# Final norm and the first projections behind an MLP, made by halves of the positions, the second half first

## The chip, the cores and the metric

The kernel runs on one core of one Trainium2 chip. The metric is the device time of one execution in microseconds; smaller is better. The kernel before took 2222.27 us in the median of 3 runs (2221.69 to 2226.16).

## The reference, cut to what matters

Two blocks run one after the other on 1024 positions of 1024 channels in float32. The first ends with a squared-ReLU MLP, its residual, and a norm; the second begins with a norm, a modulation and a wide input projection. Between the two stands the part that the change touches:

```python
h = h + squared_relu_mlp(rms_norm(h, mlp_norm[i]), mlp_w_up[i], mlp_w_down[i])
return rms_norm(h, final_norm)                       # end of the first block
...
h = _modulate(_rms(x, norm1_g[l]), sh1, sc1)         # h * (1 + scale) + shift
p = h @ w_in[l]                                      # 512 of its columns feed _fourier
...
y = jnp.fft.fft2(fg, axes=(1, 3), norm="ortho").real # positions x 128 channels, 4 groups
```

## The kernel before, in words

**Data.** Activations lie transposed: channels on the 128 partitions in 8 blocks, positions along the free dimension. `X` is the residual, 8 blocks of 1024 positions; "half 0" is positions 0 to 511 and "half 1" 512 to 1023, which is also what one PSUM bank of 512 float32 holds. Every large matmul is written as three (lines 99 to 101), on operands that are split into a `hi` part (made by ScalarE, "ACT") and a `lo` part (made by VectorE, "DVE"). `U` is the normed and modulated input of the projections, as such a pair.

**The end of the MLP.** The down projection runs as 7 passes of 8 steps, s = 0 to 55. A step is 4 blocks d of 6 matmuls, 24 in all. The four blocks of a pass accumulate in banks 0 to 3 or in banks 4 to 7, in turn: the sixth pass (s = 40 to 47) in 0 to 3, the last one (s = 48 to 55) in 4 to 7. Steps 54 and 55 are interleaved, block by block, so that block d of the last pass is done after 12 matmuls each. DVE makes the lo parts of the weights three steps ahead of TensorE (`make_lo`), and in its own step s = 48 + d adds block d of the sixth pass to `X` from its bank (`evict`, line 1765, two instructions). In the same steps ACT squares finished blocks of `X` (twice, plain and with the gain `GF`), and DVE adds the squares up in `sq` and `sqg` (line 1774). Half 1 of `X` is complete earlier than half 0: its squares belong to steps 41 to 45, those of half 0 to steps 49 to 52 and to the four blocks of the last pass.

**The norm.** `final_pe` sums the squares over channels by matmul (line 1855, 16 short ones a half; one matmul of float32 in the program is two instructions on TensorE), ACT takes roots (line 1873), DVE makes a diagonal matrix of the reciprocals (lines 1914, 1916), and a matmul with ones turns it into a row of 512 factors on all partitions (line 1862). Then for each of the 8 blocks of `X`: `t` on DVE (`X` times scale times row, line 1903), `hi` on ACT (plus shift, line 1868), `lo` on DVE (line 1908). All of that stands behind the last matmul of the MLP. Block 0 is made by halves, blocks 1 to 7 at full width.

**The projections and the Fourier part.** `four_pe` projects four groups g of 128 channels with the weight tiles `T_F[g]`: 48 matmuls for a group, 24 for one half. It makes groups 0 and 1 together, chunk by chunk as `U` comes, then group 2, then `over_channels(0)` and `(1)`, group 3, and from there position and channel transforms in turn. ACT and DVE feed them in fixed orders: ACT copies one bank of a group (`second`, line 1995), DVE folds, ACT and DVE split the result (line 2001), and so on. Behind it the gates' projections begin.

**What sets the order.** Each engine runs its list in program order; a wait on a semaphore stops all that is behind it on that engine. A PSUM bank is taken by `claim(pe, b)`, which waits for the marks that `hand_over(b, ...)` left when the bank was last filled. The queue of SyncE loads weight tiles as their buffers come free, GpSimd's queue stores finished blocks of `X` and loads small tables.

Of the kernel before, what the change touches and what calls it, by code (L numbers as in the profile page):

```python
# [103 lines left out]
def _program(nc, A, out, ctx):  # L104
# [1648 lines left out]
    def down_dve(dve):  # L1753
# [91 lines left out]

    def u_mark(k, i=1):
        return fn.dve("lo", 0, i) if k == 0 else fn.dve("lo", k)

    def final_pe(pe):
        for i in range(2):  # L1850
            claim(pe, fs_b[i])
            for name, s, c, w in (("n3", sq[0], 0, INV_EPS), ("n3g", sqg[0], 1, INV1024)):
                pe.wait_ge(*ml.dve(name, "add", i, 7))
                for tb in range(4):
                    m = pe.e.matmul(psum[:, fs_b[i], 2 * tb + c:2 * tb + 2], s[:, (4 * i + tb) * P:(4 * i + tb + 1) * P],
                                    w, start=(c, tb) == (0, 0), stop=(c, tb) == (1, 3), skip_group_check=True)
            m.then_inc(*fn.pe.one("sums", i))
            hand_over(fs_b[i], 1, fn.act("sd1", i))
        claim(pe, f_rb, 2)
        for i in range(2):  # L1860
            pe.wait_ge(*fn.dve("dg", i))
            pe.e.matmul(bank(f_rb + i), ones[:], dg[:, 4 * i:4 * i + 4, :].rearrange("p a b -> p (a b)"),
                        start=True, stop=True).then_inc(*fn.pe.one("row", i))
        hand_over(f_rb, 2, fn.dve("t", 7))

    def final_act(act):
        def hi(k, x, *step):
            act.e.activation(U[0][:, k, x], tmp[k % 2][:, x], ACT.Identity, bias=SH1[:, k:k + 1]).then_inc(
                *fn.act.one("hi", k, *step))

        for i in range(2):
            act.wait_ge(*fn.pe("sums", i))
            act.e.activation(s2[:, 4 * i:4 * i + 4], psum[:, fs_b[i], 1:8:2], ACT.Sqrt, bias=EPSEPS).then_inc(
                *fn.act.one("sd", i))
        for i in range(2):
            act.wait_ge(*fn.dve("t", 0, i))
            hi(0, half(i), i)
        for i in range(2):
            act.e.activation(s1[:, 4 * i:4 * i + 4], psum[:, fs_b[i], 0:8:2], ACT.Sqrt, bias=EPSV).then_inc(
                *fn.act.one("sd1", i))  # L1880
        for k in range(1, 8):
            act.wait_ge(*fn.dve("t", k))
            hi(k, slice(0, 1024))
# [14 lines left out]

    def final_dve(dve):
        e = dve.e  # L1900

        def t(k, x, *step):
            e.scalar_tensor_tensor(tmp[k % 2][:, x], X[:, k, x], SCF[:, k:k + 1], two(f_rb)[:, x], ALU.mult,
                                   ALU.mult).then_inc(*fn.dve.one("t", k, *step))

        def lo(k, x, *step):
            dve.wait_ge(*fn.act("hi", k, *step))
            e.scalar_tensor_tensor(U[1][:, k, x], tmp[k % 2][:, x], SH1[:, k:k + 1], f(U[0][:, k, x]), ALU.add,
                                   ALU.subtract).then_inc(*fn.dve.one("lo", k, *step))

        for i in range(2):
            c = slice(4 * i, 4 * i + 4)
            dve.wait_ge(*fn.act("sd", i))
            e.reciprocal(r2[:, c], s2[:, c]).then_inc(*fn.dve.one("rs", i))
            dve.wait_ge(*fn.dve("rs", i))
            e.tensor_tensor(dg[:, c, :], ident_rows(4), by_block(r2[:, c], 4), ALU.mult).then_inc(
                *fn.dve.one("dg", i))
        for i in range(2):
            dve.wait_ge(*fn.pe("row", i))
            t(0, half(i), i)  # L1920
        lo(0, half(0), 0)
        for k in range(1, 9):
            if k < 8:
                if k > 1:
                    dve.wait_ge(*u_mark(k - 2))
                t(k, slice(0, 1024))
            if k == 1:
                lo(0, half(1), 1)
                dve.wait_ge(*fn.act("sd1", 1))
                e.reciprocal(r1, s1).then_inc(*fn.dve.one("r1"))  # L1930
            else:
                lo(k - 1, slice(0, 1024))
# [35 lines left out]
    def four_pool(pool):  # L1968
# [180 lines left out]
    def four_pe(pe):  # L2149
# [26 lines left out]
        def project(g):  # L2176
            w = use(pe, T_F[g])
            claim(pe, g_b[g], 2)
            for i in range(2):
                for k in range(8):  # L2180
                    m = mm3(pe.e, bank(g_b[g] + i), cols(w, k, 128), ch(U, k, 512 * i, 512 * i + 512), k == 0, k == 7)
            m.then_inc(*fo.pe.one("f", g))

        ws = [use(pe, T_F[g]) for g in range(2)]
        for g in range(2):
            claim(pe, g_b[g], 2)
        for k in range(8):
# [1872 lines left out]
```

## Time and profile before

| what | value |
|---|---|
| median of 3 runs | 2222.27 us |
| the profiled execution | 2221.08 us |
| its span | 2219.0 us |
| TensorE busy | 2143.2 us, 97% |
| DVE busy | 1634.1 us, 74% |
| ACT busy | 1123.2 us, 51% |

The chain that ended last is TensorE for 82% of the span, DVE for 10% and ACT for 5%. "PEclk" in a view is the granted clock of TensorE as a share of 2.4 GHz: 1.00 is that, 0.50 is 1.2 GHz. In a timeline a matmul of 512 columns shows 0.39 us, but one starts every 0.227 us at the full clock: the starts tell the pace.

### The profile page before, as it was taken

The page shows a single profiled execution, that of the slowest core. Times are in us where ns is not written, and L with a number is a line of the kernel's source. Part 1 is how long each engine was busy: PE and PEld are TensorE (multiplying, and loading weights), DVE is VectorE, ACT ScalarE, POOL GpSimd, SP SyncE. Part 2 cuts the span into 40 slices and gives each one's busy share as a digit, 9 for nine tenths or more (in the row PEclk, how much of TensorE's full clock was granted, in tenths as well). Part 3 has the DMA queues.
Part 4 walks back from the last instruction along what each step waited for, and adds up shares of the span by engine and source line. Part 5 has one row for each costly group of instructions (what it writes and reads, how often), then busy time and mean ns, then how long its engine had stood idle before and what let it go on. Part 6 is the DMA issues. An engine that isn't in the chain of part 4 may idle for free.

```text
span 2219.0 us, 28129 instructions
## 1 busy us (share of the span) xinstructions
PE 2143.2 (97%) x10948; PEld 1789.3 (81%) x10948; DVE 1634.1 (74%) x2537; ACT 1123.2 (51%) x1725; POOL 188.3 (8%) x269
## 2 busy tenths in 40 slices
PE   8999999999999999999999999999998999899997
PEld 6898787788888888878888988788887885688885
DVE  7777457988987987986343263688887746699996
ACT  6777435444443434444322242576766312588874
POOL 0011100000001000000110032000000100111111
PEclk9999999999999999989999999999999999899998
DMA  4122712644469998652343112000001703899996
GB/s 151 48 68 85 258 74 89 216 170 176 179 242 400 384 336 281 221 127 76 124 143 99 38 48 82 10 1 1 1 20 39 280 29 141 345 392 384 378 384 221
DMA packets 114532, 373.99 MB, mean 169 GB/s; under 512 B 13360, under 2 KB 13648, under 8 KB 112736
## 3 DMA queue, kind: packets, MB, share of 16 engines
q1 hardware_dynamic: 86544, 273.00, 33.5%
q0 software_dynamic: 26704, 95.01, 13.1%
q10 hardware_dynamic: 1152, 4.19, 0.5%
q8 instruction: 86, 1.41, 0.3%
q14 instruction: 46, 0.38, 0.1%
HBM read 302.94 MB, written 69.21 MB: 168 GB/s over the span
## 4 chain that ended last, share of the span: by engine, by line
PE 82%; DVE 10%; ACT 5%; issue 1%; DMA 1%; POOLq 0%; SPq 0%; ACTq 0%; DVEq 0%
PE psum L99 24%; PE psum L100 24%; PE psum L101 24%; PE psum L3008 3%; PE psum L3019 2%; DVE w_lo L281 2%; ACT MP_hi L3109 1%; ACT PB L3075 1%; PE psum L1017 1%; DVE MP_lo L3202 1%; PE psum L990 1%; DVE small L3155 1%; PE psum L3848 1%; PE psum L3575 1%; DVE idx L3548 1%
## 5 line engine op out<-in xcount | busy, mean ns | idle before, releaser
L272 ACT ACTIVATE w_hi<-rawe 128x1024 fp32r<-128x1024 f32 x211 | 217.8, 1056 | 152.7 <-PE psum L101 78.7
L99 PE MATMUL psum<-U_hi,w_hi 128*128 128x512 f32 x688 | 271.7, 395 | 12.2 <-DVE w_lo L281 10.5
L281 DVE TENSOR_TENSOR w_lo<-rawe,w_hi 128x1024 fp32r<-128x1024 f32 x211 | 249.5, 1218 | 37.5 <-ACT w_hi L272 37.0
L100 PE MATMUL psum<-U_lo,w_hi 128*128 128x512 f32 x688 | 269.9, 392 | 0.0
L101 PE MATMUL psum<-U_hi,w_lo 128*128 128x512 f32 x688 | 269.3, 391 | 0.0
L281 DVE TENSOR_TENSOR w_lo<-raw,w_hi 128x1024 fp32r<-128x1024 f32 (+2 forms) x175 | 194.5, 1120 | 87.6 <-ACT w_hi L272 87.3
L272 ACT ACTIVATE w_hi<-raw 128x1024 fp32r<-128x1024 f32 (+2 forms) x176 | 169.0, 967 | 92.3 <-PE psum L101 55.5
L99 PE MATMUL psum<-B_hi,w_hi 128*128 128x512 f32 x448 | 176.2, 393 | 6.0 <-ACT cbuf L1433 4.3
L100 PE MATMUL psum<-B_lo,w_hi 128*128 128x512 f32 x448 | 175.3, 391 | 0.0
L101 PE MATMUL psum<-B_hi,w_lo 128*128 128x512 f32 x448 | 175.3, 391 | 0.0
L99 PE MATMUL psum<-w_hi 128*128 128x512 f32 x448 | 174.3, 389 | 0.0
L100 PE MATMUL psum<-w_lo,w_hi 128*128 128x512 f32 x448 | 174.3, 389 | 0.0
L101 PE MATMUL psum<-w_hi,w_lo 128*128 128x512 f32 x448 | 174.3, 389 | 0.0
L99 PEld LDWEIGHTS psum<-U_hi,w_hi 128*128 128x128 f32 x688 | 130.2, 189 | 39.4 <-DVE w_lo L281 10.7
L101 PEld LDWEIGHTS psum<-U_hi,w_lo 128*128 128x128 f32 x688 | 130.2, 189 | 28.0
L100 PEld LDWEIGHTS psum<-U_lo,w_hi 128*128 128x128 f32 x688 | 130.3, 189 | 25.2 <-issue 0.2
L3202 DVE TENSOR_TENSOR MP_lo<-psum,MP_hi 128x512 fp32r<-128x512 f32 x160 | 109.5, 685 | 53.6 <-ACT MP_hi L3109 53.0
L3109 ACT ACTIVATE MP_hi<-psum 128x512 fp32r<-128x512 f32 x160 | 95.6, 597 | 82.7 <-PE psum L3008 82.3
L3008 PE MATMUL psum<-ident,PB 128*128 128x128 f32 x640 | 100.4, 280 | 9.3 <-DVE MP_lo L3202 4.9
L99 PE MATMUL psum<-w_hi,xe_hi 128*128 128x512 f32 x256 | 103.9, 406 | 3.7 <-DVE hv L3803 2.7
L99 PEld LDWEIGHTS psum<-B_hi,w_hi 128*128 128x128 f32 x448 | 84.7, 189 | 24.5 <-issue 5.0
L3008 PEld LDWEIGHTS psum<-ident,PB 128*128 128x128 f32 x640 | 73.8, 141 | 35.1 <-DVE MP_lo L3202 9.4
(490 smaller groups left out, 5135.6 us busy)
## 6 DMA issues: line engine op xcount, KB each, us to landing
rawe<-in_w_e SPq DMA_DIRECT2D x112, 512.0 KB, 17.5
rawe<-in_w_dn SPq DMA_DIRECT2D x70, 512.0 KB, 6.4
rawx<-in_w_e SPq DMA_DIRECT2D x56, 512.0 KB, 18.0
rawe<-ta SPq DMA_DIRECT2D x43, 512.0 KB, 7.3
ta<-cbuf SPq DMA_DIRECT2D x64, 256.0 KB, 2.5
raw<-in_w_dn SPq DMA_DIRECT2D x26, 512.0 KB, 6.5
ta<-rg SPq DMA_DIRECT2D x48, 256.0 KB, 2.0
raw<-in_w_e SPq DMA_DIRECT2D x24, 512.0 KB, 17.6
```

What stands on the lines that cost most here:

```text
L99: e.matmul(o, l[0], r[0], start=first, stop=False, skip_group_check=skip)
L100: e.matmul(o, l[0], r[1], start=False, stop=False, skip_group_check=skip)
L101: return e.matmul(o, l[1], r[0], start=False, stop=last, skip_group_check=skip)
L272: act.e.activation(hi, src, ACT.Copy).then_inc(w_hi, 1)
L281: dve.e.tensor_tensor(lo, src, f(hi), ALU.subtract).then_inc(w_lo, 1)
L990: m = pe.e.transpose(bank(B_T[u % 2], 256 * h + P * i, 256 * h + P * i + P), EX[j % 2][:, s + i, h, P - P * i:2 * P - P * i], ident[:])
L1017: m = pe.e.matmul(psum[:, B_L + h, o + c0:o + 256], qst[(j + 1) % 2][h][:, n * P:n * P + P], kst[h][x][:, k0:n * P + P], start=x == 0, sto ...
L3008: m = pe.e.transpose(bank(t_bank("turn", n), 256 * kb + P * i, 256 * kb + P * i + P), PB[(2 * u + i) % 5][:, (2 * t + kb) * P:(2 * t + kb ...
L3019: m = pe.e.matmul(bank(B_MO, 0, 256), VV[:, 2 * y + kb, v // 4, :], MP[n0 % 4][x][:, 256 * kb:256 * kb + 256], start=(y, kb, x) == (0, 0, ...
L3075: act.e.activation(PB[m % 5][:], s_of(m), ACT.Exp, bias=nmx[:, m % 8:m % 8 + 1], accum_out=msum(c)[:, z:z + 1]).then_inc(*at_s.act.one("ex ...
L3109: act.e.activation(MP[n % 4][0][:], bank(t_bank("turn", n)), ACT.Copy).then_inc(*at_s.act.one("turn", n))
L3202: dve.e.tensor_tensor(lo[:], bank(t_bank("turn", n)), f(hi[:]), ALU.subtract).then_inc(*at_s.dve.one("turn", n))
```

## The change

- **Sums and row of half 1 move into the last pass.** `final_sums(pe, 1)` stands ahead of step 52, `final_row(pe, 1)` ahead of the interleaved steps 54 and 55. ACT's roots follow its squares of step 52, DVE's diagonal its sums of step 52. Both halves' sums now use one bank, 2; the row of half 1 uses bank 0, that of half 0 bank 6.
- **`U` is made by halves**, half 1 first, with buffers `th` of 512 in place of `tmp` of 1024. Four chunks of half 1 are made between the last evictions of the MLP, the other four behind them, then the eight of half 0.
- **The projections are made by halves.** Groups 0 and 1 of half 1 together, with the sums of half 0 behind chunk 3; the row of half 0; groups 2 and 3 of half 1; then half 0 of groups 0, 1, 2, the two channel transforms, and half 0 of group 3.
- **The tiles `T_F[2]` and `T_F[3]`** are split inside the norm, not behind it. The groups' banks change from 4, 6, 2, 0 to 2, 4, 6, 0.
- The table for the root is loaded by ACT in step 51, not ahead of the last squares.

```diff
@@ down_act
+            if s == 51:
+                act.e.activation(vec[:, 122:123], EPSV, ACT.Sqrt)
+            if s == 52:
+                final_root(act, 1)
+        u_hi(act, 0, 1)
+        u_hi(act, 1, 1)
         for d in range(4):
-            if d == 3:
-                act.e.activation(vec[:, 122:123], EPSV, ACT.Sqrt)
             squares(0, 4 + d)
+            if d < 2:
+                u_hi(act, 2 + d, 1)
@@ down_dve
+            if s == 52:
+                final_diag(dve, 1)
+        u_t(dve, 0)
+        u_t(dve, 1)
+        u_lo(dve, 0)
         for d in range(4):
             evict(6, d, 0)
             adds(0, 4 + d)
+            if d < 2:
+                u_t(dve, 2 + d)
+                u_lo(dve, 1 + d)
+            if d == 1:
+                u_lo(dve, 3)
@@ down_pe
         for s in range(N_S - 2):
+            if s == 52:
+                final_sums(pe, 1)
             for d in range(4):
                 m = step(s, d, s % 8)
...
+        final_row(pe, 1)
@@ the norm
-    g_b = [4, 6, 2, 0]
-    f_rb, fs_b = g_b[3], (g_b[2], g_b[2] + 1)
+    g_b = [2, 4, 6, 0]
+    f_rb, fs_b = (6, 0), 2
+    th = [at(f"th{i}", [512], O_V + (44 + 2 * i) * KB) for i in range(2)]
+    U_ORDER = [(k, i) for i in (1, 0) for k in range(8)]
...
+    def final_sums(pe, i):
+        claim(pe, fs_b)
+        for name, s, c, w in (("n3", sq[0], 0, INV_EPS), ("n3g", sqg[0], 1, INV1024)):
+            pe.wait_ge(*ml.dve(name, "add", i, 7))
+            for tb in range(4):
+                m = pe.e.matmul(psum[:, fs_b, 2 * tb + c:2 * tb + 2], s[:, (4 * i + tb) * P:(4 * i + tb + 1) * P],
+                                w, start=(c, tb) == (0, 0), stop=(c, tb) == (1, 3), skip_group_check=True)
+        m.then_inc(*fn.pe.one("sums", i))
+        hand_over(fs_b, 1, fn.act("sd1", i))
+
+    def final_row(pe, i):
+        claim(pe, f_rb[i])
+        pe.wait_ge(*fn.dve("dg", i))
...
+    def project(pe, gs, i, after=None):
+        ws = [use(pe, T_F[g]) for g in gs]
+        for g in gs:
+            claim(pe, g_b[g] + i)
+        for k in range(8):
+            pe.wait_ge(*u_mark(k, i))
+            for g, w in zip(gs, ws):
+                m = mm3(pe.e, bank(g_b[g] + i), cols(w, k, 128), ch(U, k, 512 * i, 512 * i + 512), k == 0, k == 7)
+            if after and k == 3:
+                after(pe, 0)
+        return m
+
     def final_pe(pe):
...
+        project(pe, (0, 1), 1, final_sums)
+        final_row(pe, 0)
+        project(pe, (2,), 1)
+        project(pe, (3,), 1)
...
+    def u_hi(act, k, i):
+        act.wait_ge(*fn.dve("t", k, i))
+        if (k, i) == (0, 1):
+            act.wait_ge(*ml.pe("d", 52))
+        if (k, i) == (4, 1):
+            act.wait_ge(*ml.pe("dn", 6, 3))
+        act.e.activation(U[0][:, k, half(i)], th[k % 2][:], ACT.Identity, bias=SH1[:, k:k + 1]).then_inc(
+            *fn.act.one("hi", k, i))
...
     def final_act(act):
+        u_hi(act, 4, 1)
+        u_hi(act, 5, 1)
+        make_hi(act, T_F[2])
+        u_hi(act, 6, 1)
+        u_hi(act, 7, 1)
+        final_root(act, 0)
+        make_hi(act, T_F[3])
+        for k in range(8):
+            u_hi(act, k, 0)
...
+    def u_t(dve, n):
+        k, i = U_ORDER[n]
+        if k == 0:
+            dve.wait_ge(*fn.pe("row", i))
+        if n > 1:
+            dve.wait_ge(*u_mark(*U_ORDER[n - 2]))
+        dve.e.scalar_tensor_tensor(th[n % 2][:], X[:, k, half(i)], SCF[:, k:k + 1], bank(f_rb[i]), ALU.mult,
+                                   ALU.mult).then_inc(*fn.dve.one("t", k, i))
...
     def final_dve(dve):
+        u_t(dve, 4)
+        for n in range(5, 8):
+            u_t(dve, n)
+            u_lo(dve, n - 1)
+        u_lo(dve, 7)
+        make_lo(dve, T_F[2])
+        final_diag(dve, 0)
+        make_lo(dve, T_F[3])
+        u_t(dve, 8)
+        for n in range(9, 16):
+            u_t(dve, n)
+            u_lo(dve, n - 1)
...
@@ the Fourier part
-        pool.wait_ge(*fn.pe("sums", 1))
+        pool.wait_ge(*fn.pe("sums", 0))
         pool.e.dma_start(cdr[:], A["dft_c"]).then_inc(cd_in.sem, 16)
...
-        project(2)
+        for g in range(3):
+            project(pe, (g,), 0).then_inc(*fo.pe.one("f", g))
         over_channels(0)
         over_channels(1)
-        project(3)
+        project(pe, (3,), 0).then_inc(*fo.pe.one("f", 3))
```

On TensorE, at the border between steps 51 and 52, the kernel before has (`w_hi` and `w_lo` are the split weights and activations; rows with `w_hi` on both sides belong to the MLP, and the second row is the first of step 52):

```order
L101 MATMUL psum<-w_hi,w_lo 128x512
L99 MATMUL psum<-w_hi 128x512 [waits w_lo_made]
L100 MATMUL psum<-w_lo,w_hi 128x512
L101 MATMUL psum<-w_hi,w_lo 128x512
L99 MATMUL psum<-w_hi 128x512
```

and the changed kernel, at the same place:

```order
L101 MATMUL psum<-w_hi,w_lo 128x512
L1879 MATMUL psum<-vec,sq_102 128x2 [waits mlp_dve]
L1879 MATMUL psum<-vec,sq_102 128x2 x3
L1879 MATMUL psum<-vec,sqg_179 128x1 x4
L99 MATMUL psum<-w_hi 128x512 [waits w_lo_made]
```

The sums of half 1 now stand between the two steps, with one wait on a count of DVE's (`mlp_dve`), and every matmul of the MLP behind them is queued behind that wait.

On DVE, from the sums of step 52 (the first two rows) to the second block of the last pass, the kernel before has:

```order
L1774 TENSOR_TENSOR sq_102<-sq_102,sq_103 128x512 [waits mlp_dve,mlp_act]
L1774 TENSOR_TENSOR sqg_179<-sqg_179,sqg_180 128x512 [waits mlp_dve,mlp_act]
L1774 TENSOR_TENSOR sq_102<-sq_102,sq_104 128x512 [waits mlp_dve,mlp_act]
L1774 TENSOR_TENSOR sqg_179<-sqg_179,sqg_180 128x512 [waits mlp_dve,mlp_act]
L281 TENSOR_TENSOR w_lo<-raw_61,w_hi 128x1024 [waits w_hi_made]
L281 TENSOR_TENSOR w_lo<-raw_59,w_hi 128x1024 [waits w_hi_made]
L1765 TENSOR_TENSOR X<-X,psum 128x512 [waits mlp_products]
```

and the changed kernel, from the diagonal that follows the same two rows:

```order
L1953 RECIPROCAL st<-st 128x4 [waits final_norm_act]
L1955 TENSOR_TENSOR dg<-ident,st 128x512 [waits final_norm_dve]
L1780 TENSOR_TENSOR sq_102<-sq_102,sq_104 128x512 [waits mlp_dve,mlp_act]
L1780 TENSOR_TENSOR sqg_179<-sqg_179,sqg_180 128x512 [waits mlp_dve,mlp_act]
L281 TENSOR_TENSOR w_lo<-raw_61,w_hi 128x1024 [waits w_hi_made]
L281 TENSOR_TENSOR w_lo<-raw_59,w_hi 128x1024 [waits w_hi_made]
L1964 SCALAR_TENSOR_TENSOR th_181<-X,modb,psum 128x512 [waits final_norm_products]
L1964 SCALAR_TENSOR_TENSOR th_182<-X,modb,psum 128x512
L1970 SCALAR_TENSOR_TENSOR U_lo<-th_181,mod,U_hi 128x512 [waits final_norm_act]
L1771 TENSOR_TENSOR X<-X,psum 128x512 [waits mlp_products]
```

The diagonal came in ahead of the last sums of a step, and two `t` and a `lo` between the weight tiles and the first eviction of the last pass.

## Rows read from the trace of the kernel before

**Rows 1.** Timeline of TensorE: start us, us, engine line op names [idle <-releaser].

```profile
940.80 0.39 PE L99 MATMUL psum<-w_hi 128*128 128x512 f32 x1
...
962.34 0.39 PE L101 MATMUL psum<-w_hi,w_lo 128*128 128x512 f32 x1
966.65 1.02 PE L1855 MATMUL psum<-vec,sq 128*128 128x2 f32 x8 [3.93 <-DVE sq L1774]
...
972.53 3.76 PE L1862 MATMUL psum<-dg,ones 128*128 128x512 f32 x4
977.89 0.77 PE L99 MATMUL psum<-U_hi,w_hi 128*128 128x512 f32 x1 [1.59 <-DVE U_lo L1908]
```

**Rows 2.** Windows there: length, PE, PEld, DVE, ACT, POOL busy (x), PEclk, DMA, GB/s.

```profile
967.00:968.00 1.00, 1.00 (x10) 1.00 (x10) 0.12 (x1) 0.00 (x0) 0.00 (x0) 0.84 0.75 299
...
981.00:982.00 1.00, 1.00 (x5) 0.84 (x4) 1.00 (x1) 1.00 (x1) 1.00 (x2) 0.83 0.00 0
```

**Rows 3.** Timeline of DVE in the last pass (columns as Rows 1).

```profile
942.62 1.28 DVE L1765 TENSOR_TENSOR X<-X,psum 128x512 f32<-128x512 f32 x2
...
954.32 2.35 DVE L281 TENSOR_TENSOR w_lo<-raw,w_hi 128x1024 fp32r<-128x1024 f32 x2
956.60 0.68 DVE L1765 TENSOR_TENSOR X<-X,psum 128x512 f32<-128x512 f32 x1
957.97 0.69 DVE L1774 TENSOR_TENSOR sq<-sq,sq 128x512 f32<-128x512 f32 x1 [0.70 <-ACT sq L1725]
```

**Rows 4.** Timeline of ACT in the last pass.

```profile
951.94 2.01 ACT L272 ACTIVATE w_hi<-raw 128x1024 fp32r<-128x1024 f32 x2 [1.44 <-PE psum L101]
...
963.77 1.28 ACT L1744 ACT_TABLE_LOAD   x1
965.06 0.20 ACT L1744 ACTIVATE vec<-vec 128x1 f32<-128x1 f32 x1
```

**Rows 5.** Instructions on tile tmp: durations ns min/median/max, starts, forms.

```profile
L1903 DVE SCALAR_TENSOR_TENSOR tmp<-X,modb,psum x9: 747/1280/1281, 974.6 to 992.2; 128x1024 f32<-128x1024 f32 x7, 128x512 f32<-128x512 f32 x2
L1868 ACT ACTIVATE U_hi<-tmp,mod x9: 722/1154/1157, 975.4 to 993.5; 128x1024 fp32r<-128x1024 f32 x7, 128x512 fp32r<-128x512 f32 x2
L1908 DVE SCALAR_TENSOR_TENSOR U_lo<-tmp,mod,U_hi x9: 744/1279/1284, 977.0 to 994.7; 128x1024 fp32r<-128x1024 f32 x7, 128x512 fp32r<-128x512 f32 x2
```

**Rows 6.** Timeline of TensorE, an earlier norm: sums, then two rows.

```profile
345.63 1.95 PE L420 MATMUL psum<-vec,sq 128*128 128x1 f32 x16
...
368.47 1.88 PE L1623 MATMUL psum<-n2dg,ones 128*128 128x512 f32 x4
```

**Rows 7.** Timeline of TensorE, two other gaps.

```profile
351.06 0.76 PE L99 MATMUL psum<-B_hi,w_hi 128*128 128x512 f32 x1 [3.48 <-ACT cbuf L1433]
...
1929.71 0.47 PE L99 MATMUL psum<-w_hi,xe_hi 128*128 128x512 f32 x1 [2.72 <-DVE hv L3803]
```

**Rows 8.** Windows around these two gaps (columns as Rows 2).

```profile
349.00:350.00 1.00, 0.00 (x0) 0.00 (x0) 1.00 (x3) 1.00 (x3) 0.00 (x0) 0.94 0.63 225
...
356.00:357.00 1.00, 1.00 (x5) 0.77 (x4) 1.00 (x3) 0.20 (x1) 0.00 (x0) 0.65 0.00 0
...
1930.00:1931.00 1.00, 1.00 (x4) 0.84 (x3) 0.59 (x1) 0.00 (x0) 0.00 (x0) 0.62 1.02 406
...
1933.00:1934.00 1.00, 1.00 (x5) 0.77 (x4) 0.66 (x1) 0.31 (x1) 0.00 (x0) 0.67 1.01 401
```

**Rows 9.** Timeline of the Fourier part, ACT's rows and the gates' first matmul.

```profile
1001.61 0.60 ACT L1995 ACTIVATE f2nd<-psum 128x512 f32<-128x512 f32 x1 [4.75 <-PE psum L101]
...
1005.14 1.06 ACT L2001 ACTIVATE FF_hi<-ff 128x1024 fp32r<-128x1024 f32 x1 [0.85 <-DVE ff L2085]
...
1007.93 1.06 ACT L2001 ACTIVATE FF_hi<-ff 128x1024 fp32r<-128x1024 f32 x1 [1.12 <-DVE ff L2085]
...
1009.49 1.99 ACT L272 ACTIVATE w_hi<-raw 128x1024 fp32r<-128x1024 f32 x2
1012.49 0.60 ACT L1995 ACTIVATE f2nd<-psum 128x512 f32<-128x512 f32 x1 [1.01 <-PE psum L101]
1012.98 0.17 ACT L2010 ACTIVATE small<-psum 128x3 f32<-128x3 f32 x1
...
1046.34 0.40 PE L99 MATMUL psum<-U_hi,w_hi 128*128 128x512 f32 x1
```

More of the change, by code:

```diff
@@ L1844, in _program @@
-    s1, r1, s2, r2 = (st[:, i, 0:8] for i in range(4))
-    def u_mark(k, i=1):
-        return fn.dve("lo", 0, i) if k == 0 else fn.dve("lo", k)
-    def final_pe(pe):
[L1850 to L1864, printed above, removed]
@@ L1866, in final_act @@
-    def final_act(act):
[L1867 to L1883, printed above, removed]
+    g_b = [2, 4, 6, 0]
@@ new lines, in _program @@
+    f_rb, fs_b = (6, 0), 2
+    th = [at(f"th{i}", [512], O_V + (44 + 2 * i) * KB) for i in range(2)]
+    U_ORDER = [(k, i) for i in (1, 0) for k in range(8)]
+    fn.pe.plan(("sums", 1), ("row", 1), ("sums", 0), ("row", 0))
+    fn.act.plan(("sd", 1), ("sd1", 1), *[("hi", k, 1) for k in range(8)], ("sd", 0), ("sd1", 0),
+                *[("hi", k, 0) for k in range(8)])
+    fn.dve.plan(*[("mod", i) for i in range(6)], ("scf",), ("rs", 1), ("dg", 1))
+    for n, y in enumerate(U_ORDER):
+        if n == 8:
+            fn.dve.plan(("rs", 0), ("dg", 0))
+        fn.dve.plan(("t", *y))
+        if n % 8 and n != 4:
+            fn.dve.plan(("lo", *U_ORDER[n - 1]))
+        if n in (3, 7, 15):
+            fn.dve.plan(("lo", *y))
@@ new lines, in final_row @@
+    def final_row(pe, i):
+        claim(pe, f_rb[i])
+        pe.wait_ge(*fn.dve("dg", i))
+        pe.e.matmul(bank(f_rb[i]), ones[:], dg[:, 4 * i:4 * i + 4, :].rearrange("p a b -> p (a b)"),
+                    start=True, stop=True).then_inc(*fn.pe.one("row", i))
+        hand_over(f_rb[i], 1, fn.dve("t", 7, i))
+    def project(pe, gs, i, after=None):
[9 more added lines that the diff above has]
+        return m
@@ new lines, in final_pe, with final_root @@
+    def final_pe(pe):
+        project(pe, (0, 1), 1, final_sums)
+        final_row(pe, 0)
+        project(pe, (2,), 1)
+        project(pe, (3,), 1)
+    def final_root(act, i):
+        c = slice(4 * i, 4 * i + 4)
+        act.wait_ge(*fn.pe("sums", i))
+        act.e.activation(s2[:, c], psum[:, fs_b, 1:8:2], ACT.Sqrt, bias=EPSEPS).then_inc(*fn.act.one("sd", i))
+        act.e.activation(s1[:, c], psum[:, fs_b, 0:8:2], ACT.Sqrt, bias=EPSV).then_inc(*fn.act.one("sd1", i))
+    def u_hi(act, k, i):
[6 more added lines that the diff above has]
+            *fn.act.one("hi", k, i))
@@ L1897, in modulation @@
         e.tensor_tensor(SCF, SC1, GF, ALU.mult).then_inc(*fn.dve.one("scf"))
-    def final_dve(dve):
[L1900 to L1932, printed above, removed]
@@ new lines, in u_lo @@
+    def u_lo(dve, n):
+        k, i = U_ORDER[n]
+        dve.wait_ge(*fn.act("hi", k, i))
+        dve.e.scalar_tensor_tensor(U[1][:, k, half(i)], th[n % 2][:], SH1[:, k:k + 1], f(U[0][:, k, half(i)]), ALU.add,
+                                   ALU.subtract).then_inc(*fn.dve.one("lo", k, i))
+    def final_dve(dve):
+        u_t(dve, 4)
[10 more added lines that the diff above has]
+            u_lo(dve, n - 1)
+        u_lo(dve, 15)
+        dve.wait_ge(*fn.act("sd1", 0))
+        dve.e.reciprocal(r1, s1).then_inc(*fn.dve.one("r1"))
@@ L2174, in over_positions @@
             hand_over(g_b[g], 2, fo.dve("y", g))
[L2176 to L2187, printed above, removed]
-            for i in range(2):
-                pe.wait_ge(*u_mark(k, i))
-                for g in range(2):
-                    m = mm3(pe.e, bank(g_b[g] + i), cols(ws[g], k, 128), ch(U, k, 512 * i, 512 * i + 512),
-                            k == 0, k == 7)
-        m.then_inc(*fo.pe.one("f", 1))
-        project(2)
+        for g in range(3):
+            project(pe, (g,), 0).then_inc(*fo.pe.one("f", g))
         over_channels(0)
         over_channels(1)
-        project(3)
+        project(pe, (3,), 0).then_inc(*fo.pe.one("f", 3))
         over_positions(0)
```

27 lines of the change are left out of this document (14 added, 13 removed).

## The prediction

> **What bounds the kernel now.** I read the page first: TensorE is busy for 97% of the span, so a gain has to come out of its idle or slow time. The list of TensorE's waits and the windows of 40 us show one such place near the change. The timeline of TensorE there [rows 1] shows a matmul of the MLP every 0.227 us until 962.34, then an idle stretch, the sums, the rows, and the first projection at 977.89. The next matmul could have started at 962.57, so 15.3 us are lost. They are a chain over all engines: DVE's last sum, 32 short matmuls, roots, diagonal, rows, `t`, `hi`, `lo`. The windows [rows 2] add the clock: it leaves 1.00 near 967.7, is 0.50 behind that, and is back near 981.2. The first 3.3 us of the projections thus ran at 1.2 GHz, which costs half of it, 1.7 us. **The loss before is 17.0 us.** From 978 to 1046.34, where the gates begin [rows 9], TensorE shows no idle time, so I compare one stretch in both kernels: from 940.80, the first matmul of step 52, to the gates' first matmul. Useful matmuls in it are the same in both.
>
> **Sums and row.** The 16 short matmuls of one half cost 1.8 us at the full clock, by an earlier norm (1.95 us for 16, with the latency of the last) [rows 6]; two rows there took 1.88, so one costs 0.9. Before, they are in the 15.3 us. Now each stands in TensorE's queue at the full clock: 2 x 1.8 + 2 x 0.9 = 5.4 us. That is paid in any case.
>
> **The new wait at step 52.** `final_sums(pe, 1)` claims bank 2. Its last user is block 2 of the sixth pass, and DVE empties it in its own step 50: the two evictions start at 942.62 and end at 943.90 [rows 3]. TensorE comes to this place at 940.80 [rows 1], since in each of DVE's steps the eviction stands behind two weight tiles and the sum for a later one. Its sums of squares of half 1 are long complete; the one wait in the listing is therefore the bank. **TensorE stands for 3.1 us**, with all of steps 52 to 55 queued behind it. DVE is busy without a pause there, and nothing in the change makes it faster ahead of 943.9. Bounds: 0 if the bank were free, 3.1 by these two rows. I take 3.1, as both times come from one timeline. A matmul may not be moved past it.
>
> **The DVE chain behind it.** Step 53 ends at 943.9 + 1.8 + 10.9 = 956.6. ACT splits `T_F[0]` only when step 53 is done [rows 4], and DVE's list hangs on that: the lo part of the first tile starts 1.3 us later (latency and one ACTIVATE of about 1.05), then two tiles 2.3 (2.35 for the pair), then four chunks of `U` and four rounds of eviction and sums. A `t` or `lo` of 512 shows 0.75 [rows 5] and takes 0.66 in a row; eight of them and two short waits for ACT are 5.7 us. A round is 0.6 for the eviction, 0.76 of waiting for ACT's square (0.70 shown) and 1.2 for two additions, 2.57 us, as before [rows 3]; four are 10.3. So the last sum of squares is there 19.7 us behind step 53, at 976.3. TensorE in the meantime has the row (0.9), steps 54 and 55 (10.9) and four chunks of groups 0 and 1 (5.4), 17.2 us, and is at the sums of half 0 at 973.8. **It waits 2.4 us.** Behind the sums, chunk 4 of `U` is late by 0.4 (its `t` is queued behind the additions), chunks 5 to 7 come every 1.43 us where TensorE wants one in 1.36, and the diagonal is late by 0.1: 0.7 in all. Then the cover is ample: groups 2 and 3 of half 1 take 10.9 us while DVE makes the eight chunks of half 0 at 1.43 each, with the first there after 2.
>
> **The Fourier part.** Group 1 is now complete only 5.4 us ahead of `over_channels(0)`, where it was 10.9. ACT's list is `second(1)`, split and copies of groups 0 and 1, two weight tiles, `second(2)`, and then the copy that the second half of `over_channels(0)` needs. By the rows of before [rows 9] that is 3.5 us from the first copy to the split (1001.61 to 1005.14), 1.56 to the tiles, 1.9 for them, 0.5 and 0.25 for the last two: 7.9 us behind group 1, and TensorE asks at 6.8. It waits 1.05. The same laying out of the queues, with 24 matmuls in place of 48 ahead of the position transforms, gives two later waits, 0.5 for the same copy of group 3 and 0.4 for the last split. Together 2.0; bounds 0 and 4.
>
> **Sum without the clock.** 5.4 + 3.1 + 2.4 + 0.7 + 2.0 = 13.6 us lost after, 17.0 before: 3.4 us gained. The same laying out of the queues for the kernel before puts its gates within 0.1 us of 1046.34.
>
> **The clock.** Three places show what it does when TensorE's dense work pauses. Before, dense matmuls end at 962.7 and the clock falls 5 us later, in the midst of short matmuls [rows 1, 2]. At 345.63, 16 short matmuls and 3.48 us of idle time [rows 6, 7]: it falls at 349.9 and is back at 356.7, 5.6 us after the restart [rows 8]. At 1929.71, a gap of 2.72 us alone [rows 7]: it falls at 1930.4 and is back at 1933.7 [rows 8]. The new kernel has two such pauses: idle 3.1 and sums 1.8 at step 52, and idle 2.4, sums 1.8, idle 0.4 behind chunk 3. Both are 4.6 to 4.9 us without dense work, between the first two examples. I take a fall in each, with 3.4 us at 1.2 GHz: 1.7 us at step 52, all of it on the path, and 1.4 to 1.5 in the chunks (a little is hidden in their waits). **3.4 - 3.2 = 0.2 us gained.**
>
> **Covered at no cost.** Loads of `T_F` tiles are issued in the last pass and used 20 us later; without that cover each would cost its landing, some us. GpSimd loads the channel table behind the sums of half 0, at 978, and ACT uses it near 999. ACT's table load moves out of the last round into step 51, where ACT waits for DVE for 1.5 us; the load took 1.28 and the next ACTIVATE began at once [rows 4], just as the eviction it needed was done, so I book 0.1 at most. The Trainium skill, "ScalarE: Activation LUTs", section "What ACT_TABLE_LOAD costs", counts a drain of 1.38 us beside the 1.283 us of the load. By that the move would save up to 1.4 us more of the last round. The rows show no such drain between 963.77 and 965.06, so the row decides.
>
> **Rivals.**
> 1. Only one of the two pauses brings the clock down: 1.8 us gained, 2220.4. For it: where the fall lies within a pause differs by over a microsecond between the examples.
> 2. The clock stays: 3.4 gained, 2218.8. Against it: all three pauses of 2.7 us or more in [rows 1, 7] ended in a fall.
> 3. **Slower.** Each fall lasts as from 349.9 to 356.7, 6.8 us. It takes 3.4 us a time, and with both the change costs 2.6 us: 2224.9. It decides from 7 us of half rate in all (3.4 / 0.5). For it: one of three examples is so long.
> 4. The wait for bank 2 isn't there, because the evictions of the sixth pass come earlier in the new run: without it one fall goes as well and 3.1 + 1.7 us come back, 2217.2; with no fall at all 2216.0. Against it: nothing ahead of step 50 is changed on DVE.
> 5. The change does what it describes and the norm is hidden but for sums and rows: 17.0 - 5.4 = 11.6 us gained, 2210.7. Against it are the 3.1 and the 2.4 us above.
>
> The Trainium skill has the rule for 1 to 3 in "TensorE: Matmul & The Clock Gate", section "Why this matters for your kernels": idle gaps between bursts of matmuls drop the array to half its clock. [...]
>
> **How the numbers follow.** The profiled execution took 2221.08 us, 1.2 below the median of the runs shown, 2222.27. The sum is made in its span and gives 2220.9; set against the median it is 2222.1. All times above are against the median. Chances: forecast 0.47, rival 1 0.25, rival 2 0.07, rival 3 0.08, rival 4 0.05, rival 5 0.03, and 0.05 for something slower that I don't see. A measurement of this kernel tells about 0.2%, 4.4 us, from no change. Faster by more: rivals 4 and 5 and a part of 2, whose bounds reach there, 0.1. Slower by more: the unseen 0.05 and the upper end of rival 3, 0.08. The rest, 0.82, is the same. The range goes from rival 2 with half a microsecond for the unknown waits, 2218.3, to rival 3, 2225.0.
>
> **What would show it.** In the profile after: the first L1879 matmul starts 3.1 us behind the last one of step 51, released by DVE's eviction L1771; the second group of L1879 waits 2.4 us for DVE's sum L1780; the clock is 0.50 for some 3.4 us behind each; the gates' first matmul stands within 1 us of where it was, seen from step 52's place. Wrong would be: no wait at the first L1879 (the term of 3.1), none at the second (the DVE chain), no 0.50 near them (the clock), or idle time in the channel transforms of over 2 us.

## The result, and the profile after

The changed kernel takes 2229.03 us (median of 8 runs, 2227.42 to 2230.92) against 2221.63 us for the kernel before on the same chip (8 runs, 2220.07 to 2226.16). The ratio is 1.0029, 95% interval [1.002, 1.0038]. The change costs 7.4 us, where 0.2 us of gain was forecast.

The profiled execution took 2229.53 us, 8.45 more than the one of before. Three marks split this. Step 52's place in TensorE's queue comes at 942.7 in place of 940.8, 1.9 us later, before anything of the change has run; it goes with more time at half rate between 220 and 250 us and changes from execution to execution (in `e3_order` below, the same code up to there, it comes at 940.3). From there to the gates' first matmul it is 112.3 us where it was 105.5: **6.8 us, the change**. Behind the gates both kernels take the same (1172.6 us before and 1172.5 after, to the end of the span).

First the waits of TensorE in the changed kernel between 930 and 1080 us (columns: who waited for whom, us in total, times, longest).

```profile
PE psum L1879 <- DVE X L1771: 3.1, 1, 3.1
PE psum L1879 <- DVE sq L1780: 2.0, 1, 2.0
PE psum L99 <- ACT small L2066: 0.9, 1, 0.9
PE psum L99 <- DVE U_lo L1970: 0.8, 1, 0.8
```

Then its timeline there, the rows that answer to [rows 1] and the last of [rows 9].

```profile
945.99 1.84 PE L1879 MATMUL psum<-vec,sq 128*128 128x2 f32 x8 [3.09 <-DVE X L1771]
947.68 1.84 PE L1879 MATMUL psum<-vec,sqg 128*128 128x1 f32 x8
...
961.92 1.02 PE L1887 MATMUL psum<-dg,ones 128*128 128x512 f32 x2
...
981.30 1.02 PE L1879 MATMUL psum<-vec,sq 128*128 128x2 f32 x8 [2.00 <-DVE sq L1780]
982.19 1.03 PE L1879 MATMUL psum<-vec,sqg 128*128 128x1 f32 x8
...
984.02 0.80 PE L99 MATMUL psum<-U_hi,w_hi 128*128 128x512 f32 x1 [0.80 <-DVE U_lo L1970]
...
1023.07 0.33 PE L99 MATMUL psum<-cd_hi,FF_hi 128*128 128x128 f32 x1 [0.86 <-ACT small L2066]
...
1055.01 0.40 PE L99 MATMUL psum<-U_hi,w_hi 128*128 128x512 f32 x1
```

The idle chain of 15.3 us is gone. In its place are four short waits, 6.8 us together. The first is the one for bank 2: DVE's eviction, the row that answers to the first of [rows 3], runs until 945.8.

```profile
944.56 1.28 DVE L1771 TENSOR_TENSOR X<-X,psum 128x512 f32<-128x512 f32 x2
```

The windows of 2 us tell the rest (columns as in rows 2: length, busy time of PE, PEld, DVE, ACT and POOL with instructions, PEclk, DMA share, GB/s).

```profile
944.00:946.00 2.00, 0.01 (x1) 0.05 (x1) 2.00 (x4) 1.32 (x2) 0.00 (x0) 0.94 0.00 0
946.00:948.00 2.00, 2.00 (x10) 2.00 (x10) 2.00 (x2) 1.98 (x4) 0.53 (x1) 0.50 0.40 158
...
952.00:954.00 2.00, 2.00 (x9) 1.54 (x9) 2.00 (x3) 0.73 (x3) 0.00 (x0) 0.85 0.98 395
...
982.00:984.00 2.00, 1.22 (x11) 1.13 (x11) 1.83 (x3) 1.54 (x3) 0.48 (x1) 0.83 0.21 86
984.00:986.00 2.00, 1.98 (x5) 1.59 (x6) 1.96 (x3) 1.51 (x2) 0.06 (x1) 0.50 0.25 74
...
990.00:992.00 2.00, 2.00 (x10) 1.59 (x10) 0.82 (x1) 0.00 (x0) 0.00 (x0) 0.96 0.82 248
...
1022.00:1024.00 2.00, 1.14 (x10) 1.00 (x10) 1.84 (x2) 1.02 (x4) 0.00 (x0) 1.00 0.19 29
1024.00:1026.00 2.00, 2.00 (x13) 2.00 (x12) 0.08 (x1) 1.14 (x3) 0.00 (x0) 0.57 0.78 211
...
1034.00:1036.00 2.00, 2.00 (x9) 1.58 (x9) 0.91 (x1) 0.00 (x0) 0.00 (x0) 0.87 0.00 0
```

Read the PEclk column. TensorE is at 1.2 GHz from 945.8 to 952.6, from 983.3 to 990.1 and from 1024.3 to 1034.5. The first stretch, worked out: the fall takes (1 - 0.94) x 2 x 2 = 0.24 us of the window from 944, three whole windows follow, and 0.6 us of the one from 952, in all 6.8 us. Windows of 0.25 us give 6.82, 6.83 and 10.24 us, 23.9 us together, which costs **11.9 us at the rate of one half that the prediction used, nearly all of it on the path**. The account of the 112.3 us: 88.5 of useful work (105.5 less 17.0), 5.4 for sums and rows, 6.8 of waits, 11.9 for the clock: 112.6.

Two small errors nearly cancel in it. In the stretches a matmul of 512 columns starts every 0.427 us (1031.13, then 1031.56) against 0.227 outside, so 47% is lost and not half, and 0.9 us of the 23.9 lie within waits: an estimate from these rows is 10.8 us. And a view counts a wait from the modelled end of the matmul ahead of it, 0.16 us behind the next slot, so the four waits cost 7.4. With these two the sum is 112.1.

### The profile page after: what moved, and what is told of

The parts are those of the page before. It is cut to its first block, busy times and chain, and to the rows that moved or that the text cites. A ratio compares the mean times of both kernels' runs of the same rounds, so it can differ in the third digit from the quotient of the medians.

```text
span 2227.5 us, 28153 instructions
## 1 busy us (share of the span) xinstructions
PE 2150.7 (97%) x10948; PEld 1796.5 (81%) x10948; DVE 1637.0 (73%) x2551; ACT 1125.0 (51%) x1732; POOL 188.2 (8%) x269
## 4 chain that ended last, share of the span: by engine, by line
PE 82%; DVE 10%; ACT 5%; issue 1%; DMA 1%; POOLq 0%; SPq 0%; ACTq 0%; DVEq 0%
PE psum L99 24%; PE psum L100 24%; PE psum L101 24%; PE psum L3047 3%; PE psum L3058 2%; ACT MP_hi L3148 1%; ACT PB L3114 1%; DVE w_lo L281 1%; PE psum L1017 1%; DVE MP_lo L3241 1%; PE psum L990 1%; DVE small L3194 1%; PE psum L3887 1%; PE psum L3614 1%; DVE idx L3587 1%
## 5 line engine op out<-in xcount | busy, mean ns | idle before, releaser
L99 PE MATMUL psum<-U_hi,w_hi 128*128 128x512 f32 x688 | 273.3, 397 | 11.7 <-DVE w_lo L281 10.8
```

The source lines that it names most:

```text
L99: e.matmul(o, l[0], r[0], start=first, stop=False, skip_group_check=skip)
```

## The experiments

Each kernel was timed beside the kernel before on the same chip. The changed kernel itself was timed on one chip alone; the kernel before took 2221.63 us there and 2222.45 to 2222.61 on the chips of the runs below, so a difference to 2229.03 is uncertain by about 1 us. Since the time at half rate elsewhere in the program changes from execution to execution, the table gives the stretch from step 52's place to the gates' first matmul, and the time at half rate in it, from one profile each.

| kernel | stretch, us | at 1.2 GHz in it, us | median of all runs, us |
|---|---|---|---|
| before | 105.5 | 13.7, most of it in the idle chain | 2221.6 to 2222.6, by chip |
| changed | 112.3 | 6.8, 6.8, 10.2 | 2229.03 |
| `e1_bank1` | 105.9 | 6.8, 10.2 | 2222.93 |
| `e2_fill52` | 106.2 | 3.4, 6.8 | 2220.49 |
| `e3_order` | 112.4 | 6.8, 3.4, 6.8 | 2229.18 |
| `e4_bank1_order` | 108.3 | 6.8, 10.2 | 2223.25 |
| `e5_fill_all` | 105.9 | 3.4, 3.4 | 2221.72 |
| `e6_e_early` | 106.0 | 6.8, 3.4 | 2223.17 |
| `e7_bank1_e` | 101.1 | 6.8 | 2216.35 |
| `e8_bank1_e_fill0` | 98.6 | none | 2214.87 |
| `e9_before_e` | 105.5 | 13.7 | 2222.59 |
| `e10_fill_behind` | 100.8 | 3.4 | 2216.82 |
| `e11_fill52_e` | 105.4 | 3.4, 6.8 | 2220.06 |

### e1_bank1: the wait for bank 2 taken away

```
-    f_rb, fs_b = (6, 0), 2
+    f_rb, fs_b = (6, 0), (2, 1)
```

and `fs_b[i]` wherever `fs_b` stood, so that the sums of half 1 go into bank 1. In this run's trace DVE has emptied it at 940.2, 1.5 us before TensorE comes to step 52 at 941.7 (the 3.5 us of the expectation below is too much).

> The changed kernel with one edit: the sums of half 1 go to bank 1, which was emptied 3.5 us before TensorE comes to step 52, instead of bank 2. Theory (pauses and the clock): the wait of 3.1 us at the first L1879 is gone, and with it the first stretch at half rate (6.8 us, worth 3.4), so the kernel takes 6.5 us less than the changed kernel, 2222.5 us. Rival (the chain of DVE sets the time anyway, the wait only hides in it): at most 3 us less, 2226 or more, with the wait come back at the row or at the sums of half 0.

Measured: 2222.93 us (10 runs), ratio to before 1.0003 [0.9993, 1.0013]. The wait and the first stretch of half rate are both gone; the stretch of the program is 6.4 us shorter. So this one wait of 3.1 us cost twice its length. The expectation was met within 0.4 us. The third stretch was still there, behind the same short wait as in the changed kernel:

```profile
1015.64 0.33 PE L99 MATMUL psum<-cd_hi,FF_hi 128*128 128x128 f32 x1 [0.86 <-ACT small L2066]
```

### e2_fill52: the wait kept, dense matmuls in it

```
             if s == 52:
+                claim(pe, 1)
+                for _ in range(3):
+                    pe.e.matmul(bank(1), ident[:], sq[0][:, half(1)], start=True, stop=True)
                 final_sums(pe, 1)
```

These matmuls compute nothing that is used.

> The changed kernel with bank 2 and its wait kept, and three extra float32 matmuls of 512 columns into the empty bank 1 ahead of the first sums: useless work of about 2.6 us inside the 3.1 us in which TensorE would stand idle. Theory (the clock falls since TensorE pauses): the sums still start behind the eviction, but the clock stays at 1.00 there and 3.4 us come back, 2225.6 us. Rival (the half rate isn't caused by that pause): no change, 2229.0 us, or slower.

Measured: 2220.49 us (10 runs), ratio 1.0001 [0.9991, 1.0011], and two groups of times: six from 2218.5 to 2220.7, four from 2223.7 to 2226.5. The gain is larger than expected. In the profile, one of the fast group, the first stretch was 3.4 us in place of 6.8, and the third was absent, though its wait was there, among the same matmuls:

```profile
1019.72 0.33 PE L99 MATMUL psum<-cd_hi,FF_hi 128*128 128x128 f32 x1 [0.85 <-ACT small L2069]
```

The shorter first stretch is in all three profiles with this filler (this one, `e5_fill_all`, `e11_fill52_e`), and 6.8 us in all three that have the wait without it (the changed kernel, `e3_order`, `e6_e_early`). Filling the wait thus shortened the half rate behind it. What governs the third stretch this run doesn't tell: the wait of 0.85 us was not enough by itself.

### e3_order and e4_bank1_order: a projection moved to cover group 1

```
         for g in range(3):
             project(pe, (g,), 0).then_inc(*fo.pe.one("f", g))
+        project(pe, (3,), 0).then_inc(*fo.pe.one("f", 3))
         over_channels(0)
         over_channels(1)
-        project(pe, (3,), 0).then_inc(*fo.pe.one("f", 3))
```

The prediction held that group 1 comes too close ahead of `over_channels(0)`; this puts 24 matmuls between them. The second kernel has the edit of `e1_bank1` too.

> The changed kernel with the projection of group 3, half 0, put ahead of the two channel transforms instead of behind them. Theory: the wait of 0.9 us for ACT's small copy goes, since 5.4 us of dense work now cover it, and the third stretch at half rate (10.2 us, worth 5.1) goes with it: 6 us less, 2223.0 us. Rival (the channel transforms with their 128-column matmuls bring the clock down by themselves, wherever they stand): 1 us less, 2228 us, with a fall of the clock in them.

> Both edits, bank 1 for the sums of half 1 and group 3 ahead of the channel transforms. Theory: the two gains add up, 12.5 us less than the changed kernel, 2216.5 us, some 5 us faster than the kernel before; one pause and one fall are left, at the sums of half 0. Rival (later stages or DVE take the gain back): 2221 us or more.

Measured: 2229.18 us (7 runs), ratio 1.003 [1.0018, 1.0041], and 2223.25 us (10 runs), 1.0004 [0.9994, 1.0013]. Neither gain came; the edit gains nothing on either kernel. Waits of TensorE in `e3_order`:

```profile
PE psum L99 <- DVE FF_lo L2146: 2.8, 1, 2.8
PE psum L2210 <- ACT alt L2061: 1.1, 1, 1.1
```

The wait of 0.9 us went, but the projection had been the cover for ACT and DVE later on, and 3.9 us of waits came up there, with half rate for 6.8 us behind the longer one (10.2 us in `e4_bank1_order`, from the midst of the same wait). A cover moved is a cover taken away somewhere else.

### e5_fill_all: all three pauses filled

As `e2_fill52`, with two such matmuls ahead of the sums of half 0 and

```
+                if n == 4 and g == 0:
+                    claim(pe, 0)
+                    for _ in range(6):
+                        pe.e.matmul(bank(0), cd[0][:, 0:128], x[0][:, 0:512], start=True, stop=True)
                 if n == 4:
                     pe.wait_ge(*fo.act("e", g))
```

> The changed kernel with useless dense matmuls in each of its three pauses: three fp32 ones of 512 columns ahead of the sums of half 1 (0.86 us each, 2.6 in a wait of 3.1), two of them ahead of the sums of half 0 (1.7 in 2.0), and six of 512 columns at 0.23 us ahead of the fifth block of the first channel transform (1.4 in 0.9). No wait is taken away. Theory (the 7.4 us lost are the three half-rate stretches of 6.8, 6.8 and 10.2 us, each set off by a pause): all three gone, 11.9 given back, 0.5 paid for the last filler: 2217.6 us, 0.2% under the kernel before. Rival 1 (the third stretch comes from the narrow matmuls of the channel transforms and not from the pause): it stays, 5.1 less is given back: 2222.7. Rival 2 (the stretches come whatever stands in the pauses): 2229.5.

Measured: 2221.72 us (11 runs, 2219.09 to 2223.74), ratio 0.9994 [0.9985, 1.0003]. The median lies nearest to rival 1, but the profile says otherwise: the third stretch is gone, and the other two are there with 3.4 us each (this execution took 2219.45). So 7.3 us came back where the theory gave 11.4. What the fillers left is telling: three of them left 0.5 us of the wait for the bank, and half rate for 3.4 us came from 947.9 on, 3.3 us behind its end. Rival 2 falls. Since the first two stretches didn't go fully, the theory holds in direction and not in size.

### e6_e_early: the third wait taken away without useless work

```
+        one(0)
+        second(2)
         make_hi(act, T_DFT[1])
-        second(2)
-        one(0)
         z(0)
```

The list of marks is put in the same order. `one(0)` is the copy (L2066) for which the fifth block of the first channel transform waits. In the changed kernel it stood behind the rounding of a weight tile (two ACTIVATEs) and the copy L2051; ACT's timeline of the changed kernel:

```profile
1020.40 1.99 ACT L272 ACTIVATE w_hi<-raw 128x1024 fp32r<-128x1024 f32 x2
1022.30 0.57 ACT L2051 ACTIVATE f2nd<-psum 128x512 f32<-128x512 f32 x1
1022.77 0.15 ACT L2066 ACTIVATE small<-psum 128x3 f32<-128x3 f32 x1
```

> The changed kernel with one edit on ScalarE: the copy of the 3-column sums of group 0 (L2066), on which the fifth block of the first channel transform waits 0.86 us, moves ahead of the rounding of a weight tile (2.0 us) and of the second copy. Theory (the pause sets off the third stretch): the wait (0.9) and the stretch (10.2 us at half rate, 5.1 lost) both go: 2223.0 us. Rival (the narrow matmuls set it off, or it only moves): the wait alone goes: 2228.1 us, and a stretch of 6.8 or 10.2 us stands somewhere between 1015 and 1045 us.

Measured: 2223.17 us (11 runs), ratio 1.0003 [0.9994, 1.0012]; the theory said 2223.0. In its first two channel transforms, from 1018.3 to 1024.1, TensorE doesn't wait at all; two short waits come up later, in the transform of group 3 and behind it. Their rows, and the windows of the first two transforms, full speed where the changed kernel fell to half:

```profile
1040.34 0.33 PE L99 MATMUL psum<-cd_hi,FF_hi 128*128 128x128 f32 x1 [0.39 <-ACT small L2066]
1045.03 0.39 PE L99 MATMUL psum<-w_hi,Z_hi 128*128 128x256 f32 x1 [0.21 <-DVE Z_lo L2151]
```

```profile
1020.00:1022.00 2.00, 2.00 (x20) 2.00 (x19) 1.64 (x2) 1.91 (x3) 0.00 (x0) 1.00 0.00 0
1022.00:1024.00 2.00, 2.00 (x21) 2.00 (x19) 2.00 (x5) 0.55 (x3) 0.00 (x0) 1.00 0.61 141
```

The matmuls of 128 columns are all still there, so they alone didn't bring the clock down; with the wait of 0.86 us among them gone, the third stretch was gone. In `e2_fill52` the wait was there and the stretch was not: it took the wait, and something more that these runs don't isolate. The program's stretch is 6.3 us shorter. Some 1.6 of that is the second stretch at half rate, 3.4 us here and not 6.8; the other 4.7 are the third one, since the wait that went is nearly made up by the two that came.

### e7_bank1_e: both repairs

> Sums of half 1 in bank 1 (as in the run with that edit alone, 2222.9) and the copy on ScalarE earlier. Theory (the pause sets off the third stretch): 2222.9 - 0.9 - 5.1 = 2216.9 us, some 0.25% faster than the kernel before. Rival (narrow matmuls, or it moves): 2222.0 us.

Measured: 2216.35 us (7 runs, 2214.69 to 2216.93), ratio 0.997 [0.9959, 0.9981]: faster than both kernels, and within 0.6 us of the theory. The stretch is 4.8 us shorter than in `e1_bank1`, as near as the 4.7 above. What is left of TensorE's waits between 930 and 1065 us (the first channel transform has none; the last 0.4 and 0.2 stand at 1035.4 and 1040.1), and the windows at the two repaired places and at the one left as it was:

```profile
PE psum L1879 <- DVE sq L1780: 1.5, 1, 1.5
PE psum L99 <- DVE U_lo L1970: 0.7, 1, 0.7
PE psum L99 <- ACT small L2066: 0.4, 1, 0.4
PE psum L1887 <- DVE dg L1955: 0.4, 1, 0.4
PE psum L99 <- DVE Z_lo L2151: 0.2, 1, 0.2
```

```profile
944.00:946.00 2.00, 2.00 (x10) 1.60 (x9) 2.00 (x3) 2.00 (x3) 0.53 (x1) 1.00 0.00 0
...
974.00:976.00 2.00, 1.73 (x15) 1.73 (x16) 2.00 (x4) 0.58 (x2) 0.00 (x0) 0.98 0.65 262
976.00:978.00 2.00, 1.29 (x4) 1.10 (x5) 1.83 (x4) 2.00 (x4) 0.55 (x1) 0.50 0.08 14
...
1016.00:1018.00 2.00, 2.00 (x20) 2.00 (x20) 2.00 (x3) 1.54 (x4) 0.00 (x0) 1.00 0.11 27
```

### e8_bank1_e_fill0 and e10_fill_behind: the pause at the sums of half 0

```
             if after and k == 3:
+                claim(pe, 1)
+                for _ in range(2):
+                    pe.e.matmul(bank(1), ident[:], sq[0][:, half(1)], start=True, stop=True)
                 after(pe, 0)
```

in `e8_bank1_e_fill0`; in `e10_fill_behind` the same lines stand behind `after(pe, 0)`. Both have the two repairs.

> The same two edits and two useless fp32 matmuls of 512 columns (0.86 us each, 1.7 in a wait of 1.5) in the pause ahead of the sums of half 0. Theory (that pause sets off the stretch of 6.8 us behind it, 3.4 lost): 3.4 less than without the filler, 0.2 paid: 2213.7 us if the third stretch went too, 2218.8 if it stayed. Rival (a filler doesn't keep the clock here): 2217.1 or 2222.2 us.

> As the kernel with bank 1, the earlier copy and the filler, but the two useless fp32 matmuls of 512 columns stand behind the sums of half 0 (in the wait of 0.7 us for U_lo), and not ahead of them: the pause of 1.5 us and the narrow matmuls behind it stay as they are. Theory (the pause ahead of the sums sets the stretch off): half rate for 6.8 us as without filler; the fillers add 1.7 less the 0.7 that they fill: 2217.4 us, and up to 0.8 more where they run at half rate. Rival (dense work close behind the pause is enough to keep the clock): no half rate, 2216.35 - 3.4 + 1.0 = 2214.0 us.

Measured: 2214.87 us (6 runs, 2214.2 to 2217.19), ratio 0.9968 [0.9956, 0.998], and 2216.82 us (11 runs, 2215.2 to 2220.07), 0.9975 [0.9966, 0.9984]. With the filler ahead of the sums the clock never leaves 1.00 in the whole stretch, which is 2.5 us shorter than in `e7_bank1_e` though it has useless work in it. The windows of `e8_bank1_e_fill0` at the place:

```profile
974.00:976.00 2.00, 1.13 (x9) 1.05 (x10) 1.83 (x4) 1.82 (x3) 0.55 (x1) 1.00 0.12 43
976.00:978.00 2.00, 2.00 (x10) 1.47 (x10) 1.97 (x4) 1.28 (x3) 0.00 (x0) 1.00 0.25 66
```

A wait of 0.9 us behind the short matmuls stood in the first of these windows, and the clock stayed; what the filler took away is the wait of 1.5 us ahead of them. The medians differ by 1.5 us where the theory had 3.2, so 2214.87 lies between theory and rival, nearer to the theory. With the filler behind the sums, and the wait of 1.5 us left, the clock fell, but for 3.4 us instead of 6.8. The median, 0.5 us above that of `e7_bank1_e`, lies between the two expectations, nearer to the theory (2217.4) than to the rival (2214.0): dense work close behind the pause didn't prevent the fall. Whether it is what made the half rate shorter, one profile doesn't show, since this second stretch was also 3.4 us in `e3_order` and `e6_e_early` with no filler at all.

### e9_before_e: is the copy's place a gain by itself?

> The kernel before with only the edit on ScalarE (the copy of the 3-column sums of group 0 ahead of the rounding of a weight tile and of the second copy). Theory (the edit is worth something only behind the change, since TensorE waits nowhere in the Fourier part of the kernel before and shows no half rate there): within 0.5 us of the kernel before. Rival (the edit is a gain of its own, and the faster kernels owe it a part that the change has no share in): 0.9 us or more faster.

Measured: 2222.59 us (11 runs), ratio 1.0001 [0.9992, 1.001], against 2222.45 for the kernel before. The edit is worth nothing without the change. So the 6.3 us by which `e7_bank1_e` beats the kernel before on the same chip (2222.61 - 2216.35) are what the change is worth once the two waits that it brought are mended.

### e11_fill52_e: the two groups of times

> The changed kernel with the filler of three fp32 matmuls in the wait for bank 2 and the earlier copy on ScalarE. The kernel with the filler alone fell into two groups of times (2218.5 to 2220.7 and 2223.7 to 2226.5). Theory (the upper group is the executions in which the third stretch came): the upper group is gone and the copy's wait with it: median 2218.7 us, all below 2221.5. Rival (the groups are of another place): two groups as before, the median some 1 us under 2220.5.

Measured: 2220.06 us (11 runs, 2217.27 to 2223.24), ratio 0.9989 [0.998, 0.9998]. The times from 2223.7 to 2226.5 are gone and there are no two groups, but the median stands 1.4 us above the theory's and two runs lie above 2221.5. The upper group was thus probably the executions with the third stretch; the spread that stays is of the first two stretches, 3.4 and 6.8 us in this profile, and of places elsewhere. Why the third stretch was absent in some executions of `e2_fill52`, with its wait in place, and in none of the changed kernel as far as the narrow range of its times tells, stays open.

## Why the prediction was wrong

**What held.** The chain of 15.3 us, the 5.4 us for sums and rows (sixteen short matmuls show 1.92 us at 981.30, a row 1.02), and the wait for bank 2: 3.1 us by two rows of before, 3.09 measured, released by L1771 as written. The DVE chain was put at 2.4 and 0.7 us and measured 2.0 and 0.8. The copy in the first channel transform was put at 1.05 and measured 0.86; the two later waits of 0.5 and 0.4 didn't come in the changed kernel, but they did, as 0.4 and 0.2, in `e6_e_early` and `e7_bank1_e`, where no half rate stood ahead of them. All that without the clock: 13.6 us forecast, 12.2 measured (5.4 and the four waits). That part would have given a gain of 4.8 us.

**What failed: the term of the clock.** It was booked as two falls of 3.4 us at 1.2 GHz, 3.2 us lost. It measured three, of 6.8, 6.8 and 10.2 us, 11.9 lost at the prediction's own rate of one half (10.8 by the estimate above). By that rate the term is 8.7 us too small, the rest of the sum 1.4 too large, 7.3 us together; the stretch missed its forecast by 7.0 (6.8 longer in place of 0.2 shorter), and the 0.3 over comes of the small errors named above. Two steps made it.

1. *The length.* The prediction had three examples of a fall and took the length of the shortest, the one behind a gap alone [rows 7, 8]. But its two pauses are a wait and then sixteen short matmuls, and the example nearest in make-up, at 345.63 [rows 6, 7] (the same two parts, the short matmuls first), had lasted 6.8 us. Rival 3 said that, with 0.08; its 2.6 us of loss lies near the 2.0 that the measured waits and the first two stretches make (12.2 + 6.8 - 17.0). The nearest row by make-up should have set the term. The runs add that one length wasn't to be had from one profile in any case: the second stretch is 6.8 us in the changed kernel and 3.4 in `e3_order` and `e6_e_early`, with the same waits of 2.0 and 0.8 us, and the example at 345.63 itself, 6.8 us in twelve profiles, is 3.4 in that of `e8_bank1_e_fill0`.
2. *The third place.* The prediction put a wait of 1.05 us into the Fourier part and priced it at 1.05 us, with no term for the clock; its three examples all had pauses of 2.7 us or more. It cost 0.9 and, by the 4.7 and 4.8 us of `e6_e_early` and `e7_bank1_e`, nearly 5 more. (The medians of `e1_bank1` and `e7_bank1_e`, on two chips whose kernels before differ by 0.2, are 6.6 apart.) The wait stands in the midst of matmuls of 128 columns, twelve ahead of it and all the rest of two transforms behind. That this is what made so short a wait dear is likely, but no run separates it from the length of the wait.

The three examples were also not all. The trace of before has ten stretches at half rate that end: five of 3.4 us, three of 6.8, one of 10.2, one of 13.7. At 1698.1 a stretch of 6.8 us began between two waits of 1.16 and 1.14 us among matmuls of 128 and 256 columns. And the one of 10.2 us, from 1251.0 on, had no wait ahead of it at all, only matmuls of one column from 1248.3 on:

```profile
1248.29 1.84 PE L2485 MATMUL psum<-vec,qs 128*128 128x1 f32 x16
1249.99 3.49 PE L2485 MATMUL psum<-vec,ks 128*128 128x1 f32 x20
...
1696.66 0.66 PE L3008 MATMUL psum<-ident,PB 128*128 128x128 f32 x4 [1.16 <-DVE MP_lo L3202]
1698.45 1.12 PE L3008 MATMUL psum<-ident,PB 128*128 128x128 f32 x4 [1.14 <-DVE MP_lo L3202]
```

```profile
1250.00:1252.00 2.00, 2.00 (x16) 2.00 (x16) 0.00 (x0) 0.00 (x0) 0.00 (x0) 0.75 0.00 0
...
1698.00:1700.00 2.00, 1.12 (x4) 0.72 (x4) 2.00 (x3) 1.56 (x4) 0.00 (x0) 0.54 0.19 78
```

So the trace of before could have shown that waits near 1 us, and very short matmuls, can go with a fall, and that the length of a fall runs from 3.4 to 13.7 us.

**The range.** It reached to rival 3, 2225.0. The measured 2229.0 is rival 3 and a third fall that had no place among the cases. Without the last one, some 6 us less and 2223.2 as `e6_e_early` measured, the time would have been in it.

**The Trainium skill's rule** in "TensorE: Matmul & The Clock Gate", section "Why this matters for your kernels", that idle gaps between bursts of matmuls halve the array's clock, is given there for longer gaps than TensorE's waits of 2.0 and 0.86 us here. Read as it stands it would have priced the first pause alone, and the trace shows a fall behind all three; the measurement decides.

**The test named.** "The clock is 0.50 for some 3.4 us behind each" and "idle time in the channel transforms of over 2 us": the first was wrong as said, and the second looked for idle time where the loss was clock.

## What to carry to other kernels

When a norm or any chain is cut up and its parts are set between dense matmuls, count each new wait of TensorE with the slow stretch behind it: here taking away 3.1 us of wait gave 6.4, and the wait of 0.9 us cost nearly 6. Don't leave the short ones out, above all beside narrow matmuls, and take them away by small means, a free bank or a copy two entries earlier in ACT's list; two such edits turned 7 us of loss into 6 us of gain. Where one profile gives the length of a slow stretch, read all the stretches in it, short waits too, take them as the range of the term, and the one nearest in make-up as its value.

## What the runs showed of the hardware

All stretches at half rate in these profiles that end within the program last 3.4, 6.8, 10.2 or 13.7 us, nothing in between (132 stretches in the thirteen profiles). So the clock's part of a wait's price came in steps of some 1.6 us (47% of 3.4), whatever the wait's own length. The same code at the same place had 3.4 us in one execution and more in another: between 220 and 250 us, ahead of everything that was changed, the kernel before shows 3.4 us and the changed one two stretches of 3.4 and 6.8. A single profile of this kernel can't tell differences of 2 or 3 us between two versions for that reason; the place has to be read by itself, from mark to mark.
